# One core, DiT trunk: the context moved behind the tokens in the prologue, and MLP1's first pairs in a new written order

## The reference, cut to what matters

```python
sh1, sc1, g1, sh2, sc2, g2 = adaln(c, w_mod, b_mod, 6)       # silu(c) @ w_mod + b_mod
h  = rmsnorm(x, norm1_w) * (1 + sc1) + sh1                   # 1024 tokens
proj = h @ w_in                                              # q, k, v, z (gates), r, conv and pool columns
csh1, csc1 = adaln(c_ctx, w_mod, b_mod, 2)
hc = rmsnorm(ctx, norm1_w) * (1 + csc1) + csh1               # 256 context rows
pc = hc @ w_in[:, K_OFF:R_OFF]                               # k, v, z of the context only
s_ctx = final states of the gated linear attention over the context
x  = x + g1 * (concat(attention(from s_ctx), conv, pool) @ w_out)
h2 = rmsnorm(x, norm2_w) * (1 + sc2) + sh2
x  = x + g2 * (square(relu(h2 @ w_mlp1)) @ w_mlp2)           # 4096 hidden features
out = rmsnorm(x, final_norm_w)
```

## Time and profile before

| | us |
|---|---|
| median of 3 runs (lowest, highest) | 1088.19 (1086.53, 1090.26) |
| the profiled execution, its own time | 1089.87 |
| span of its trace, first to last instruction | 1088.0 |
| TensorE busy | 1062.0 (98%) |
| VectorE busy | 826.6 (76%) |
| ScalarE busy | 508.9 (47%) |
| GpSimd busy | 307.9 (28%) |

### The profile page before, as it was taken

One profiled execution on the slowest core, in us unless ns is written; L12 is line 12 of the kernel. 1 busy time (PEld: TensorE's weight loads), 2 busy tenths in 40 slices (PEclk: granted clock), 3 DMA queues, 4 the chain that ended last, 5 costly groups with the idle time before them and its releaser, 6 DMA issues.

```text
span 1088.0 us, 16279 instructions
## 1 busy us (share of the span) xinstructions
PE 1062.0 (98%) x5512; PEld 851.8 (78%) x5512; DVE 826.6 (76%) x1070; ACT 508.9 (47%) x818; POOL 307.9 (28%) x280
## 2 busy tenths in 40 slices
PE   8999999999999999998999999999999999999995
PEld 4578888777778888787888888888778888888884
DVE  4887869737544987799878787787987777777776
ACT  5657533356624312576666666666422222222234
POOL 1000006287301344013232323323333122222322
PEclk9999999999999999999999999999999999999998
DMA  9523240011013555225857566667746844864604
GB/s 369 225 97 116 89 142 31 31 40 40 21 40 136 231 191 216 78 78 227 315 229 273 232 257 245 239 262 284 295 168 259 334 185 184 339 253 185 256 1 155
DMA packets 58900, 199.80 MB, mean 184 GB/s; under 512 B 5600, under 2 KB 6880, under 8 KB 58336
## 3 DMA queue, kind: packets, MB, share of 16 engines
q1 hardware_dynamic: 58848, 199.11, 48.3%
HBM read 139.32 MB, written 59.77 MB: 183 GB/s over the span
## 4 chain that ended last, share of the span: by engine, by line
PE 49%; DVE 4%; issue 1%; POOL 0%; DVEq 0%; ACT 0%; ACTq 0%; POOLq 0%
PE ob L1382 13%; PE main L1424 13%; PE sm L1382 10%; PE sm L1424 8%; PE ob L1424 5%; DVE XR L2632 1%; DVE XR L2699 1%; DVE slot L2463 1%; DVE stage L2513 1%; DVE slot L2458 0%; DVE stage_last L2513 0%; DVE t_tmp L2497 0%; DVE t_tmp L2506 0%; DVE hid L2520 0%; DVE hid L2499 0%
## 5 line engine op out<-in xcount | busy, mean ns | idle before, releaser
L953 PE MATMUL main<-a_hi,w_hi 128*128 128x512 f32 x376 | 125.8, 416 | 0.0
L1382 PE MATMUL ob<-h_sum,slot 128*128 128x512 f32 x504 | 122.8, 393 | 3.0 <-DVE hid L2520 3.0
L1838 ACT ACTIVATE slot<-raw 128x512 fp32r<-128x512 f32 x80 | 50.2, 631 | 153.1 <-PE main L1424 58.4
L953 PE MATMUL main<-a_lo,w_hi 128*128 128x512 f32 x376 | 116.7, 391 | 0.0
L953 PE MATMUL main<-a_hi,w_lo 128*128 128x512 f32 x376 | 116.2, 390 | 0.0
L1382 PEld LDWEIGHTS ob<-h_sum,slot 128*128 128x128 f32 x504 | 95.7, 190 | 23.4 <-issue 3.4
L2632 DVE SCALAR_TENSOR_TENSOR XR<-main,mods,XR 128x512 f32<-128x512 f32 x112 | 83.3, 748 | 28.8 <-PE main L1424 27.7
L953 PEld LDWEIGHTS main<-a_hi,w_lo 128*128 128x128 f32 x376 | 70.6, 188 | 15.6
L953 PEld LDWEIGHTS main<-a_lo,w_hi 128*128 128x128 f32 x376 | 70.6, 188 | 15.6
L953 PEld LDWEIGHTS main<-a_hi,w_hi 128*128 128x128 f32 x376 | 66.7, 188 | 17.9 <-issue 5.8
L1424 PE MATMUL main<-t_even,slot 128*128 128x512 f32 x336 | 78.1, 389 | 0.0
(11 more groups left out here) (354 smaller groups left out, 2453.7 us busy)
## 6 DMA issues: line engine op xcount, KB each, us to landing
hidden_kept<-stage SPq DMA_DIRECT2D x98, 512.0 KB, 4.2
raw<-wstream SPq DMA_DIRECT2D x60, 512.0 KB, 4.3
t_even<-hidden_kept SPq DMA_DIRECT2D x56, 512.0 KB, 5.8
raw<-wstream SPq DMA_DIRECT2D x16, 1024.0 KB, 5.2
stage<-hidden_kept SPq DMA_DIRECT2D x21, 512.0 KB, 5.4
stage_last<-hidden_kept SPq DMA_DIRECT2D x21, 512.0 KB, 6.1
wmod<-wm SPq DMA_DIRECT2D x4, 2048.0 KB, 23.6
mbuf<-wm SPq DMA_DIRECT2D x16, 512.0 KB, 4.0
```

Of the source, the lines that this page charges most:

```text
L953: ins = pe.matmul(main[:, bank, half * HALF:(half + 1) * HALF], w[:, slot, k, :], x[:, half * HALF:(half + 1) * HALF], start=begin, stop=end)
L1382: ins = pe.matmul(hid_bank(acc, odd), slots1[j][:, w, kp, :], parts[x][:, kp, :], start=PARTS[j][3] and kp == 0 and m == 0, stop=kp == KP ...
L1838: act.activation(slots2[j][:, 0, :, :, :], operand(s, j), ACT.Copy).then_inc(w2_hi, 1)
```

## The change

It has two parts that share nothing but the kernel.

In the prologue the eight token blocks are loaded first and `ct` comes after the fourth modulation piece. The modulation weights come in eight pieces of 1 MB, one for each block k, and each is issued behind the square of block j. The squares of the tokens have places of their own (two are added on VectorE, the rest is summed on TensorE); the idle products are 10. The modulation rows use 4 column groups over 256 columns. The context's squares, root, scaling, high and low parts are taken out of the blocks' cycle and put between and behind them, and TensorE runs the context's products for G and V0 behind all token products. VectorE's order is `modulation(k)`, `scale1(k)`, one piece of other work, `low1(k)`.

In MLP1 the sums of weight quarters of pairs 2 and 3 go from GpSimd to VectorE, the lists written by hand reach to pair 4, the parts of the plain pairs stand behind the weight parts in them, a copy waits for one block of the old pair (`block_free`) and not for all, `T_ORDER` has part 4 in third place, and SP issues the load of the next weights ahead of the stores.

```diff
-T_ORDER = (0, 3, 1, 2, 5, 4, 6)
+T_ORDER = (0, 3, 4, 1, 2, 5, 6)
-GROUPS = 3
+GROUPS = 4
-FILL = (18, 2)
+FILL = (10, 2)
@@ SP
             def load_wmod(j):
-                sp.dma_start(wmod[j][:, :, :].rearrange("p k c -> p (k c)"), wm1[j]).then_inc(wmod_loaded[j], 16)
+                sp.wait_ge(sq1_made, j + 1)
+                sp.dma_start(wmod[j][:, :, :], wm1[j // 2].rearrange("p (k j c) -> p k j c", j=2, c=2 * P)[:, :, j % 2, :]
+                             ).then_inc(x_wmod_loaded[j], 16)
-            sp.dma_start(xs[:, :, N:NA], ct).then_inc(ctx_loaded, 16)
             for k in range(KT):
-                sp.dma_start(xs[:, k, 0:N], xt[k]).then_inc(x_loaded[k], 16)
+                sp.dma_start(xs[:, k, 0:N], xt[k]).then_inc(x_wmod_loaded[k], 16)
             load_wmod(0)
             sp.dma_start(wg[:, :, :].rearrange("p k c -> p (k c)"), wg_in).then_inc(wg_loaded, 16)
+            load_wmod(1)
             load_tile(0)
-            load_wmod(1)
             load_wmod(2)
             load_wmod(3)
+            sp.dma_start(xs[:, :, N:NA], ct).then_inc(ctx_loaded, 16)
+            load_wmod(4)
+            load_wmod(5)
...
+            def load_next(i, load):
+
+                sp.wait_ge(w1_lo, i * NPART - NPART)
+                load()
+
+            load_next(2, lambda: load_w1(4, 0, stream1(4)))
             for j in T_ORDER:
                 keep_hidden(0, j)
+            for i in (3, 4):
+                for j in T_ORDER:
+                    keep_hidden(i - 2, j)
+                load_next(i, lambda: load_w1(i + 2, i % 2, stream1(i + 2)))
+            for j in T_ORDER:
+                keep_hidden(3, j)
@@ POOL
-            part_sums1(2, 0, first=True)
-            part_sums1(3, 1)
             with pool.Fori(2, NMP // 2) as q:
@@ PE
+            for ready, k in (((sq1_made, 1), 0), ((sq1_made, 2), 1), ((acc1_made, 1), 2), ((acc1_made, 2), 4), ((sq1_made, 7), 6)):
+                pe.wait_ge(*ready)
+                sums_of(square_place(k), (1, 0), k == 0, False)
+            for n, half in enumerate((1, 0)):
+                pe.wait_ge(sq1_made, KT + n)
+                sums_of(square_place(7), (half,), False, True).then_inc(sums1_done, 1)
...
             pe.wait_ge(wg_split, 1)
+            gate_high(0)
+            modulation_turned(1)
+            gate_low(0)
+            value_high(0)
             modulation_rows(2)
+            value_low(0)
+            for k in range(1, KT - 1):
+                modulation_turned(k + 1)
+                gate_high(k)
+                gate_low(k)
+                value_high(k)
+                if k + 2 < KT:
+                    modulation_rows(k + 2)
+                value_low(k)
+                if k == 3:
+                    pe.wait_ge(squares_c_added, 2)
+                    for q in range(2):
+                        ins = pe.matmul(ob[:, HALF:HALF + NC], ones, squares_c[:, q, :], start=q == 0, stop=q == 1)
+                    ins.then_inc(sums_c_done, 1)
+            gate_low(KT - 1)
+            gate_high(KT - 1, last=True).then_inc(sums1_done, 1)
+            value_high(KT - 1)
+            value_low(KT - 1)
+
+            for k in range(KT):
+                pe.wait_ge(c1_hi, 2 * k + 1)
+                if k < KT - 1:
+                    context_products(k, 0, wide, wg_parts[:, k, :], c_hi, first=True)
+                pe.wait_ge(c1_lo, k + 1)
+                context_products(k, 0, narrow, wg_parts[:, k, 0:2 * RANK], c_lo)
...
@@ ACT, prologue, for each k: the high part, copy_rows(k + 1), and then
+                if k == 0:
+                    weight_high(0)
+                elif k == 2:
+                    act.wait_ge(ctx_loaded, 16)
+                    act.activation(squares_c[:, :, :], xs[:, :, N:NA], ACT.Square).then_inc(squares_c_made, 1)
...
+                elif k >= 5:
+                    for c in {5: (0, 1), 6: (2, 3), 7: (4, 5, 6, 7)}[k]:
+                        context_high(c)
@@ DVE, prologue
+            for k in range(1, KT):
+                modulation(k)
+                scale1(k)
+                if k == 1:
+                    weight_low(0)
+                elif k == 3:
+                    add_context(4)
+                elif k == 4:
+                    add_context(2)
+                elif k in (5, 6):
+                    scale_context(k - 5)
+                elif k == 7:
+                    context_low(0)
+                    context_low(1)
+                low1(k)
@@ ACT, MLP1
+            def block_free(pair, j, sums=0):
+
+                if sums:
+                    act.wait_ge(t_sum, pair * 4 + sums)
+                act.wait_ge(t_lo, pair * NPART + (T_AT[j] + 1))
+
             t_high(0, 0, 0, "first")
+            t_high(0, 0, 3, "first")
             w1_high(2, 0, 0, True)
             w1_high(2, 1, 0, True)
             plain_hidden(1, 0)
...
@@ DVE, MLP1 (n of w1_low is the place in HID_ORDER)
             sum_low(0)
             sum_low(1)
+            part_sums1(2, 0, (0, 1))
+            w1_low(2, 0, 0)
+            part_sums1(2, 0, (2,))
+            w1_low(2, 1, 0)
+            t_made(0, 0, 1, "first")
             t_low(0, 0, 0)
...
+            add_out(2, 0, 1, ACC_A, 4, 1, 1)
+            part_sums1(3, 1, (0, 1))
+            w1_low(3, 0, 1)
+            t_made(0, 0, 4, "first")
+            part_sums1(3, 1, (2,))
+            w1_low(3, 1, 1)
...
+            part_sums1(3, 1, (3,))
+            w1_low(3, 5, 1)
             t_made(1, 1, 4, "plain")
+            w1_low(3, 6, 1)
             t_low(1, 1, 5)
             t_low(1, 1, 6)
+            t_made(2, 0, 1)
+            t_low(2, 0, 0)
+            add_out(3, 1, 1, ACC_A, 4, 1, 1)
+            w1_low(4, 0, 0)
...
```

More of the change, by code:

```diff
@@ L186 @@
 BANKED = ("vt", "kt", "kc", "cs", "u", "A", "ns", "pl", "md")
-SMALL = [(_name, _j) for _j in range(KT // 2) for _name in ("rows", "turn")]
+SMALL = [(_name, _j) for _j in range(KT) for _name in ("rows", "turn")]
 for _t in range(NPROJ):
@@ L1022, in _, with sums_of @@
             pe.wait_ge(c_ready, 1)
-            def sums_of(squares, halves, with_context, first, last):
+            def sums_of(squares, halves, first, last):
                 for half in halves:
@@ L1242, in _ @@
+            for k in range(KT):
+                context_products(k, 1, slice(0, P), w_hi[:, 0, k, :], c_hi, first=True)
+                context_products(k, 1, slice(0, P), w_hi[:, 0, k, :], c_lo)
+                ins = context_products(k, 1, slice(0, P), w_lo[:, 0, k, :], c_hi, last=True)
+            ins.then_inc(tile_done, 1)
             gate_products(0)
@@ L2581, in period @@
+            t_low(3, 1, 4)
+            w1_low(4, 6, 0)
+            t_low(3, 1, 1)
+            add_out(4, 0, 1, ACC_A, 4, 1, 1)
+            w1_low(5, 0, 1)
+            t_low(3, 1, 2)
+            t_made(3, 1, 4)
+            third_out(4, 0)
+            w1_low(5, 1, 1)
+            t_low(3, 1, 5)
+            t_low(3, 1, 6)
             def period(i, odd, kind=""):
```

546 lines of the change are left out of this document (299 added, 247 removed).

## The result

| | before | changed |
|---|---|---|
| median of the runs, us | 1088.19 | 1095.34 (1093.48 to 1095.77) |
| ratio, with its 95% interval | 1 | 1.0063 (1.0051 to 1.0075) |
| profiled execution, its own time | 1089.87 | 1095.08 |
| span of its trace | 1088.0 | 1093.3 |
| TensorE busy | 1062.0 | 1060.5 |

The account below looks back on a forecast made before the run. TensorE, busy 1062.0 of 1088.0 us, was taken as the bound. Prologue -1.8 and MLP1 +2.5 gave +0.7: profiled 1089.87 becomes 1090.6, and with 1.68 off, a median of 1089.0 (range 1082.5 to 1092.8).

Parts of the forecast that it names:

- its mark: Prologue's end: the start of gate_products(0), at 67.18 us before the change, forecast 1.8 us earlier.
- The base: Starting time: the profiled execution's 1089.87 us, taken as 1.68 above the median, so 1.68 was subtracted from the forecast.
- The walk of the queues: MLP1: VectorE's and ScalarE's lists walked one instruction at a time; new stalls of 7.4 us against 4.86, +2.5 us.
- waits in front: MLP1, up to pair 3's second add_out: VectorE waits at weight parts, the add and others, together 7.1 us.
- the prediction's second estimate: MLP1: by the skill's exclusion rule each meeting costs up to 0.6 us more; pair 3's stall 3.2 instead of 2.0.
- the ring: Prologue: closed cycle of VectorE and ScalarE through modulation, scale1, high and low part; 4.1 us a block, 28.7 for seven.
- The start: Prologue: low1(0) starts near 26.9 us, 7.0 us before the old 33.89.
- TensorE's share of a block: Prologue: ten matmuls at 0.227, rows about 0.9 and a turn 0.5 make 3.7 us, inside the 4.1.
- The clock: Prologue: TensorE has little to do from 22 to 27 us; 3.4 us at half pace, 0.6 us taken off the gain.
- the prologue gives nothing: Rival, prologue: row products take 1.4 and the clock falls twice; -1.8 becomes +0.6, 1091.4 us; chance 0.11.
- Behind the mark: After the prologue: SP's later loads come 1.2 us later against the mark; VectorE's 2.3 us of idle absorbs it, cost nothing.
- clock falls on the new stalls: Rival, MLP1: stalls of pairs 3 and 4 bring the clock down, 1.7 us each; 1092.4 us; chance 0.15.

Follow-up runs that it names:

- e10: Kernel before with GpSimd's weight sums on 16 of their 512 columns, the very first excepted (hidden features not the reference's): 1083.50 us, ratio 0.9961.
- e6: e2 with GpSimd's weight sums from pair 4 on cut to 16 of 512 columns (hidden features not the reference's): 1084.66 us, ratio 0.9974.
- e5: e2 with the eight weight sums of pairs 2 and 3 back on GpSimd, so the new MLP1 order without them: 1092.43 us, ratio 1.0048.
- e9: e2 with VectorE's t_made(0, 0, 1 to 3) and t_low(0, 0, 0) put ahead of w1_low(2, 0, 0): 1091.16 us, ratio 1.0032.
- e2: Kernel before with all of the change except the prologue's part, that is MLP1's part alone: 1092.60 us, ratio 1.0037.
- e3: Changed kernel, but SP issues the fourth weight tile behind the first two blocks of the later modulation weights: 1094.16 us, ratio 1.0054.
- e12: The prologue of e4 in front of the MLP1 of e8: 1086.25 us, ratio 0.9979.
- e8: e7 with three VectorE operations moved: an add_out, the first sum of pair 3 and a t_low: 1083.77 us, ratio 0.9967.
- e1: Kernel before with only the prologue's part of the change: 1091.25 us, ratio 1.0024.
- e4: e3 plus three idle TensorE products between the first modulation rows and their turn: 1093.36 us, ratio 1.0046.
- e7: Kernel before with only the eight weight sums of pairs 2 and 3 on VectorE, all other order as before: 1085.25 us, ratio 0.9972.
- e13: e12 with scale1, the high part and low1 of blocks 1 to 7 split in two halves of 512 tokens: 1084.54 us, ratio 0.9966.

## Why the prediction was wrong, step by step

Between the forecast profiled execution, 1090.6, and the measured 1095.08 lie 4.5 us: 1.9 in the prologue up to its mark, 1.3 in the wait behind it, 0.3 in MLP1, 0.35 at MLP2's begin and 0.7 in the last transfers. The base adds the rest of the 6.3 us between the medians: 1.68 was taken off, where the changed kernel's profiled execution lies 0.26 below its median.

**MLP1: right, in place and size.** Forecast +2.5 from 7.4 us of new stalls; measured 7.65 and +2.8. The walk of the queues gave six stalls, 2.0, 0.8, 1.8, 0.7, 1.6 and 1.0; the trace has six too, as many in each pair: 2.17, 0.7, 1.1, 0.6, 1.4 and 0.9, and 0.7 spread over the products behind them. The mechanism was right too, and can now be said more simply. Between the second adds of pairs 2 and 3 (`add_out` n=1, which part 6 waits for) the changed list has 30 VectorE operations, between the next two 26, then 24; before it was 24, 21, 21 (the prediction's 22 for a pair are these 21 and the add itself). At 0.60 each, with four meetings of 1.1, 19.04 us hold (19.04 - 4.4) / 0.60 = 24. Pair 3 (two meetings) needs 18.0 + 2.2 and its waits for ScalarE, pair 4 needs 15.6 + 4.4 = 20.0: each more than 19.04, and pair 5 has nothing to pay back with. (The add is not counted in these either; with it each sum is 0.6 more, and pair 5's 14.4 + 4.4 comes to 19.4.) GpSimd's sums are what makes a pair so tight (e10 closes MLP1, e6 nearly), and postponing 13 parts is what fills it over (e5). The part that I named as waits in front (7.1 us of VectorE's waits) is nearly so in the trace, 6.1 until 531, but filling them gives nothing (e9). Not foreseen was what stands around it: in the median executions MLP1's part costs 4.45 (e2), because the clock can fall at the new stall as it did at the old. What I could have seen and didn't: the walk that I had would have told that the sums alone, in the old order, gain 3.8 us. I walked only the change as a whole.

The price of one meeting was read wrongly in the prediction's second estimate (3.2 us for the first stall). The rows at 525.46 and 527.17 take 1.1 us more than the usual 0.68. The GpSimd sums beside them end at 526.70 and 528.40, 1.24 and 1.23 us after the two operations start, and the operations end at 527.25 and 528.95, each 0.55 us behind its sum. It is so nearly everywhere in the changed kernel's MLP1: at the end of 48 of 49 sums a VectorE operation is under way, and it ends 0.54 to 0.56 us behind the sum. `add_out`, one of whose inputs is a PSUM bank of TensorE, is not held up, though a sum runs over the whole of it:

```profile
540.28 2.29 POOL L917 TENSOR_TENSOR held<-raw 128x512 f32<-128x512 f32 x1 [6.35 <-DVE slot L2572]
541.33 0.68 DVE L2657 TENSOR_TENSOR hid<-hid,sm 128x512 f32<-128x512 f32 x1
```

The Trainium skill (SBUF — State Buffer, Who interferes with whom) has a VectorE operation with two SBUF inputs and a GpSimd operation that reads SBUF exclude each other by a lock. The trace agrees: the held operation is through 0.55 us behind the sum's end. The 3.2 charged every meeting with the whole sum, but VectorE's operation starts some 0.4 us after it.

**Prologue, up to its mark: wrong, -1.8 forecast, +0.1 measured.** Three terms of the sum were off, all the same way. Two additions in it were also not what they say: the terms listed behind the root at 21.5 come to 24.8 and not 25.6, and 26.9 + 28.7 + 1.28 puts the end of the last low part at 56.9 and not 57.3. Both slips made the forecast later, so it was nearer to the trace than its own terms. (Likewise row products of 1.4 would cost the ring 0.7 us by its terms, 4.2 for 4.1 in seven blocks, and not 1.5.)
- The start: `low1(0)` at 26.9 forecast, 28.0 measured. The idle products ended at 11.8, not 11.0, as the higher clock came at 7.9 us instead of 7.1 in this execution; the root, its copy and the first high part took the rest.
- TensorE's share of a block: 3.7 forecast, 4.14 measured, 50.91 to 55.05. I had priced ten matmuls at 0.227 each; beside the row products and turns the five pairs take 2.70 instead of 2.27 (0.74 for the pair behind the row product). With VectorE's ring at 4.2, not 4.1, there was no slack in which the turn behind the context's sum of squares could hide: seven blocks took 30.9 us, not 28.7. The row product itself cost 1.00, near the 0.9 taken.
- The clock: 6.9 us at half pace, where I had taken 3.4. What it costs show e3, with this fall, whose mark stands at 67.42, and e12, with the same prologue, three idle products and no fall: 65.07. The old prologue without a fall has its mark at 65.2 to 65.6 (e2, e5, e6, e8, e10), so at full clock the new one gains 0.1 to 0.5 us.

The last low part ended at 60.15 instead of 57.3. From there the 7.1 us for the last products and the context are exact (60.21 to 67.28), and the wait of 2 us ahead of the last block is there. In size this is the rival "the prologue gives nothing" (+0.6, 11 in 100), with another cause than its row products of 1.4.

**Behind the mark: the step that failed outright.** "SP's later loads ... (1.2 us later against the mark than before), which VectorE feels at the first `add_modulation`; it has 2.3 us of idle behind that step, so nothing." The loads came at 68.33 instead of 63.32, that is 4.9 later against the mark. I had looked at the second weight split only as late by what stands ahead of the context. But in VectorE's new list it stands behind all four `zsb` copies, and SP's `load_tile(3)`, which waits for that split, stands ahead of the modulation's loads. 2.3 us of idle don't hold 4.9: 1.2 us of TensorE, shown by e3.

**The base.** I subtracted the 1.68 by which the profile of before stood above its median as if the changed kernel would have the same luck. That profile had a fall of the clock in the prologue which most executions of before don't have (three profiles of eight have it); the new prologue has its own in each of its three profiles. From the median the prologue costs 3.1 (e1), not 1.4. The rival "clock falls on the new stalls" came true in the profiles of e2 and e4, which have the same MLP1, and not in the changed kernel's own. It put the point of decision at a stall of "some 2 us"; no row gave that figure, and the runs show none: 2.15 to 2.17 us at pair 3 came with a fall in two profiles (e2, e4) and without in two (the changed kernel, e3).

So of the 7.15 us, by estimate: 1.4 prologue, most of it the queue behind it; 1.7 the clock there, which most executions of before keep up; 2.8 MLP1; 0.35 MLP2; the rest, about 1, is the last transfers (0.7 in the profile; why they take longer stays open) and MLP1's falls of the clock in some executions, which these runs do not part.

## What to carry to other kernels

Walk each part of a change alone, in the old order as well as the new: here one edit alone gains 3.7 us in the trace, 2.9 in the median (e7), and the other takes 6.5 on top of it (7.65 for 1.17), and only their sum was looked at. For a list between two fixed points of the bounding engine, count operations times spacing plus meetings against the time between the points; postponed work doesn't vanish, it lands in the next interval, which has to have room. When a step is moved on one engine, follow the loads that wait for it on SP's queue and then all that is written behind those loads. And take the profiled execution's clock falls out before it serves as the base.

## What the runs showed of the hardware

- A VectorE operation with both inputs in SBUF that meets a GpSimd sum is held until the sum ends: it finishes 0.54 to 0.56 us behind the end of 48 of 49 sums in the changed kernel's MLP1. One that reads a PSUM bank keeps its 0.68 beside a sum of 2.29.
- The same wait of TensorE is followed by the lower clock in one execution and not in another: 2.0 us at pair 3 with a fall in e2 and e4 (1.7 us more for the next products), without in the changed kernel, e3, e5 and e9 (1.7 to 2.0); 2.2 us at 58 to 60 with a fall in e1 and e4, without in the changed kernel, e3 and e12. Behind the old 3.0 us it fell in both profiles that have it, before and e1, but 18 of 75 timed executions of before have a mean clock of 0.997, as high as the profiles without any fall (e6, e12, e13). Repeated times of one kernel stand in steps of that size (e8: 1.7 us; e12: 2 to 3), and the slower ones have the lower mean clock in e12 (0.994 or 0.995 for 0.996).
- A product of 12 matmuls that follows a wait takes 2.96 to 3.06 us, not 2.88, at full clock, and the one behind it starts about 0.1 late: six waits cost 0.7 us beside themselves.
- Four column groups over 256 columns: 16 instructions in 1.00 us to the next one; 4 rounds of 0.21 would be 0.85. The fourth group runs beside the other three. The Trainium skill (TensorEngine Tiling, Key Properties) has it so.
